# A decoder trunk on one core: the gated-attention projections of heads 1 to 3 in pairs of column strips, seven block products to a pair

## The reference, cut to what matters

```python
proj = rmsnorm(h, norm_g) @ w_in                  # 1024 -> q 1024, k 1024, v 2048, gate 16, r 2048
log_a = log_sigmoid(g_low @ w_gate_up + b_gate) / 16
# 4 heads: q, k, log_a (528, 256), v and r (528, 512) each; chunked causal attention:
b = cumsum(log_a)                                  # inside a chunk
attn = where(causal, (q * exp(b)) @ (k * exp(-b)).T, 0)
o = attn @ v + (q * exp(b)) @ S                    # S carries the chunks before
y = rmsnorm(o per head) * head_norm_g * silu(r)
h = h + y @ w_out
```

## Time and profile before

| | |
|---|---|
| time, median of 2 runs | 1004.57 us (1004.5 to 1004.64) |
| span of the profiled execution | 1002.4 us |
| TensorE busy | 994.3 us, 99% of the span, 7843 instructions |
| VectorE busy | 732.4 us, 73% |
| ScalarE busy | 552.2 us, 55% |
| GpSimd busy | 90.6 us, 9%, all of it after the GLA layer |
| DMA | 107.69 MB, mean 107 GB/s |

### The profile page before, as it was taken

One profiled execution on the slowest core, in us unless ns is written; L12 is line 12 of the kernel. 1 busy time (PEld: TensorE's weight loads), 2 busy tenths in 40 slices (PEclk: granted clock), 3 DMA queues, 4 the chain that ended last, 5 costly groups with the idle time before them and its releaser, 6 DMA issues.

```text
span 1002.4 us, 19364 instructions
## 1 busy us (share of the span) xinstructions
PE 994.3 (99%) x7843; PEld 940.7 (94%) x7843; DVE 732.4 (73%) x1190; ACT 552.2 (55%) x915; POOL 90.6 (9%) x97
## 2 busy tenths in 40 slices
PE   9999999999999999999999999999999999999998
PEld 8999999999999999998889989999899989988897
DVE  6874677477567875435889976898589966989875
ACT  6754654564465554334566655656366645566633
POOL 0000000000000000000232211222112211210000
PEclk9999999999999999999999999999999999999999
DMA  8221231132122113333334432444244533486332
GB/s 293 78 71 64 67 101 45 63 103 68 64 72 97 44 63 127 105 108 104 113 82 122 108 137 60 134 103 137 89 114 110 120 117 91 124 257 233 115 106 84
DMA packets 42392, 107.69 MB, mean 107 GB/s; under 512 B 4784, under 2 KB 12848, under 8 KB 42304
## 3 DMA queue, kind: packets, MB, share of 16 engines
q1 hardware_dynamic: 41584, 105.78, 34.6%
q10 hardware_dynamic: 720, 0.68, 0.2%
HBM read 98.34 MB, written 7.90 MB: 106 GB/s over the span
## 4 chain that ended last, share of the span: by engine, by line
PE 89%; DVE 6%; ACT 2%; issue 2%; DMA 0%; DVEq 0%; ACTq 0%
PE psum L2076 50%; PE psum L2452 13%; PE psum L2371 7%; PE psum L2430 3%; PE psum L2566 3%; PE psum L2201 2%; DVE w_lo L1226 1%; PE psum L2411 1%; PE psum L2149 1%; PE psum L2573 1%; PE psum L2197 1%; PE psum L2399 1%; PE psum L2398 1%; PE psum L2400 1%; PE psum L2170 1%
## 5 line engine op out<-in xcount | busy, mean ns | idle before, releaser
L1226 DVE TENSOR_TENSOR w_lo<-raw,w_hi 128x1024 fp32r<-128x1024 f32 x156 | 191.5, 1242 | 38.3 <-ACT w_hi L682 28.0
L682 ACT ACTIVATE w_hi<-raw 128x1024 fp32r<-128x1024 f32 x156 | 162.9, 1052 | 47.8 <-PE psum L2371 29.5
L2076 PE MATMUL psum<-xh,w_hi 128*128 128x264 f32 x768 | 159.1, 288 | 0.2 <-DVE w_lo L1240 0.2
L2076 PE MATMUL psum<-xl,w_hi 128*128 128x264 f32 x768 | 155.9, 285 | 0.0
L2076 PE MATMUL psum<-xh,w_lo 128*128 128x264 f32 x768 | 155.2, 283 | 0.0
L2076 PEld LDWEIGHTS psum<-xh,w_hi 128*128 128x128 f32 x768 | 118.6, 189 | 1.6 <-issue 1.4
L2076 PEld LDWEIGHTS psum<-xl,w_hi 128*128 128x128 f32 x768 | 119.5, 188 | 0.0
L2076 PEld LDWEIGHTS psum<-xh,w_lo 128*128 128x128 f32 x768 | 119.1, 189 | 0.0
L624 POOL TENSOR_TENSOR sub<-sub,cst 128x128 f32<-128x128 f32 x64 | 50.8, 796 | 650.1 <-DMA sub<-sums 649.8
L2076 PE MATMUL psum<-y_lo,w_hi 128*128 128x264 f32 (+2 forms) x336 | 79.6, 299 | 0.0
L2452 PE MATMUL psum<-y_lo,w_hi 128*128 128x256 f32 x312 | 57.9, 287 | 0.1
(11 more groups left out here) (353 smaller groups left out, 2486.5 us busy)
## 6 DMA issues: line engine op xcount, KB each, us to landing
raw<-w_all SPq DMA_DIRECT2D x143, 512.0 KB, 3.5
sub<-sums SPq DMA_DIRECT2D x16, 264.0 KB, 7.2
y_keep<-sq SPq DMA_DIRECT2D x14, 256.0 KB, 2.2
y<-y_keep SPq DMA_DIRECT2D x14, 256.0 KB, 6.5
sub<-sums SPq DMA_DIRECT2D x16, 200.0 KB, 6.3
yr<-y_keep SPq DMA_DIRECT2D x12, 256.0 KB, 4.9
sub<-sums SPq DMA_DIRECT2D x16, 136.0 KB, 4.9
hT<-xT SPq DMA_DIRECT2D x8, 264.0 KB, 5.3
```

The costliest lines, as they stand in the source:

```text
L682: nc.scalar.activation(w_hi[:, n % HI_RING, :], raw[:, n % LO_RING, :], ACT.Copy).then_inc(hi_made, 1)
L1226: nc.vector.tensor_tensor(w_lo[:, n % LO_RING, :], raw[:, n % LO_RING, :], w_hi[:, n % HI_RING, :].bitcast(F32), ALU.subtract).then_inc(lo ...
L2076: i = nc.tensor.matmul(o, w[a][:, k % KT, :], x[b][:, k, c0:c1], start=k == first and a == b == 0, stop=k == last and a == 1)
```

## The change

Heads 1 to 3 no longer take their 36 strips one by one. Two strips form a pair (18 pairs: q, k, v, r, w, s of each head, where w and s are the second halves of v and r), and a pair's product is seen as a 2 x 2 block product: the two strips, the two halves of the 1024 features, the two halves of the tokens. Seven block products (`gp`, 4 k-tiles x 3 parts = 12 matmuls of 264 columns each) take the place of eight. Their order on TensorE is 1, then 3 of the pair before, then 2, 6, 5, 7, 4.

- **Tokens.** At the end of head 0 VectorE scales `hT` in place by gain and `rstd` (`norm_tokens`), makes four sums or differences of its quarters (`token_sum`), and ScalarE and VectorE split the quarters and the sums anew. `xT` is loaded again after the last product, as `hT` no longer holds the residual stream.
- **Weights.** Of a pair, chunks `a` and `b` are loaded; four half chunks (s1 to s4) are sums, made by DMAs of GpSimd's queue that add what they read to what lies at their destination (`pair_sums`). s1 has a buffer of its own, s3 lies in chunk `b`, and s2 and s4 make up chunk `e`, which is split like the others. ScalarE splits `e` right behind the first copy of the pair, `keep(n, 0)`.
- **Outputs.** Products 1, 6 and 7 add up in one PSUM bank, and ScalarE copies it after each of them (`keep` 0, 1, 2); 5 and 3 add up in another. VectorE makes the four output quarters (`pair_out`), each an addition of one PSUM bank and one copy.
- **Scaling.** q, k, v and r need no `rstd` any more; the 1/16 of q moves into the head's root. v's split is one instruction each instead of four.
- The order of ScalarE, VectorE and TensorE in heads 0 to 3 is rewritten around the pairs. TensorE's product `A{h}3` moves into the next head's first pair, for head 3 into the output projection.

```diff
+GP = [(x, h) for h in range(1, GLA_HEADS) for x in "qkvrws"]
+GP_STRIPS = {"q": ("Q", 0, 1), "k": ("K", 0, 1), "v": ("V", 1, 0), "r": ("R", 1, 0), "w": ("V", 3, 2), "s": ("R", 3, 2)}
+GP_BANK = {1: 2, 6: 2, 7: 2, 2: 3, 5: 0, 3: 0, 4: 1}
+GP_ORDER = []
+for _n in range(len(GP)):
+    GP_ORDER += [(1, _n)] + ([(3, _n - 1)] if _n else []) + [(p, _n) for p in (2, 6, 5, 7, 4)]
+GP_ORDER += [(3, len(GP) - 1)]
+GP_AT = {x: i + 1 for i, x in enumerate(GP_ORDER)}
...
+        GP_X = {1: (part_of(xh, 0, 0), part_of(xl, 0, 0)), 2: (part_of(xh, 1, 0), part_of(xl, 1, 0)), 3: (part_of(xh, 1, 1), part_of(xl, 1, 1)),
+                5: (th[:, 0], part_of(tl, 0, 0)), 6: (th[:, 1], part_of(tl, 0, 1)), 7: (th[:, 2], part_of(tl, 1, 0)),
+                4: (part_of(xh, 0, 1), part_of(tl, 1, 1))}
...
+                    a = w_all[AT[f"p{n:02d}a"]]
+                    s2, s4 = pair_raw(n, "e")
+                    if n == 1:
+                        sp.wait_ge(strip_made, 8)
+                        sp.wait_ge(xn_made, KT)
+                    elif n:
+                        sp.wait_ge(prod_done, GP_AT[(5, n - 2)])
+                    if n:
+                        sp.wait_ge(s1_sum, 16 * n)
+                    sp.dma_start(gs1(n)[0], w_all[AT[f"p{n:02d}b"], :, 0:CH // 2]).then_inc(s1_loaded, 16)
+                    if n < 2:
+                        wait_chunk_used(sp, m - 1 - LO_RING)
+                    else:
+                        sp.wait_ge(prod_done, GP_AT[(6, n - 2)])
+                    if n:
+                        sp.wait_ge(s2_sum, 16 * n)
+                    sp.dma_start(s2, a[:, 0:CH // 2]).then_inc(s2_loaded, 16)
+                    load(m)
+                    if n >= 2:
+                        wait_chunk_used(sp, m - 1 - LO_RING)
+                    if n:
+                        sp.wait_ge(s4_sum, 16 * n)
+                    sp.dma_start(s4, a[:, CH // 2:CH]).then_inc(s4_loaded, 16)
...
+                pool.wait_ge(s1_loaded, 16 * (n + 1))
+                pool.dma_start(s1_, from_b[:, CH // 2:CH], accum_op=ALU.add).then_inc(s1_sum, 16)
+                pool.wait_ge(s2_loaded, 16 * (n + 1))
+                pool.wait_ge(s1_sum, 16 * (n + 1))
+                pool.dma_start(s2, s1_, accum_op=ALU.add).then_inc(s2_sum, 16)
+                pool.wait_ge(w_loaded[b % LO_RING], 16 * LOADS[b])
+                if n:
+                    pool.wait_ge(s3_sum, 16 * n)
+                pool.dma_start(s3, from_a[:, 0:CH // 2], accum_op=ALU.add).then_inc(s3_sum, 16)
+                pool.wait_ge(s4_loaded, 16 * (n + 1))
+                pool.wait_ge(s2_sum, 16 * (n + 1))
+                pool.dma_start(s4, s2, accum_op=ALU.add).then_inc(s4_sum, 16)
...
+            def keep(n, i):
+                act.wait_ge(prod_done, GP_AT[((1, 6, 7)[i], n)])
+                if n:
+                    act.wait_ge(out_made, gp_out_at(n - 1, ("11", "12", "21")[i]))
+                nc.scalar.activation((u1, u2, u3[:])[i], bank(GP_BANK[1], 0, HALF), ACT.Copy, scale=(1.0, 1.0, -1.0)[i]).then_inc(copied, 1)
...
+                    n = pair("v", h)
+                    keep(n, 0)
+                    if n:
+                        pair_high(n, "e")
+                    pair_high(n, "b")
+                    decay_kb(h)
+                    decay_qb(h)
+                    keep(n, 1)
+                    pair_high(n + 1, "a")
+                    s1_high(n + 1)
+                    decays_last(h)
...
+                n = pair("w", h)
+                keep(n, 0)
+                if n:
+                    pair_high(n, "e")
+                gla_scores_hi(h)
                 gla_gate(h, 1)
-                gla_scores_hi(h)
-                ahead(f"V{h}2")
-                gla_value(h, 2)
+                pair_high(n, "b")
+                pair_high(n + 1, "a")
+                keep(n, 1)
+                s1_high(n + 1)
...
+                product, u, i = {"11": (2, u1, 0), "22": (5, u3[:], 2), "21": (4, u3[:], 2), "12": (3, u2, 1)}[name]
+                dve.wait_ge(copied, 3 * n + i + 1)
+                dve.wait_ge(prod_done, GP_AT[(product, n)])
...
+                    pair_low(n + 1, "a")
+                    pair_low(n + 1, "e")
+                    s1_low(n + 1)
+                    difs_last(h)
+                    n = pair("v", h)
+                    pair_out(n - 1, "12")
+                    pair_low(n, "b")
+                    pair_out(n, "11")
+                    mul_q64(h)
+                    first_low(n + 1)
+                    pair_out(n, "22")
+                    pair_out(n, "21")
+                    pair_low(n + 1, "a")
+                    pair_low(n + 1, "e")
+                    s1_low(n + 1)
+                    mul_qj(h)
+                    half_inverse(h - 1, 0)
+                    n = pair("r", h)
+                    pair_out(n - 1, "12")
+                    pair_low(n, "b")
+                    pair_out(n, "11")
+                    half_inverse(h - 1, 1)
+                    mul_qc(h)
+                    gla_values_lo(h, 0)
+                    muls_far(h)
+                    muls_k(h)
...
+                    head_row(h - 1, 0)
+                    head_row(h - 1, 1)
+                pair_low(n + 1, "a")
+                pair_low(n + 1, "e")
+                s1_low(n + 1)
+                if h + 1 == GLA_HEADS:
+                    y_low(0)
+                n = pair("s", h)
                 gla_out(h, 0)
...
+                x = GP_X[product]
+                o = bank(GP_BANK[product], 0, HALF)
+                for k in range(KT // 2):
+                    for a, b in PARTS:
+                        i = nc.tensor.matmul(o, w[k][a], x[b][:, k, :], start=product not in (3, 6, 7) and k == a == b == 0,
+                                             stop=k == KT // 2 - 1 and a == 1,
+                                             skip_group_check=product in (3, 6, 7))
+                i.then_inc(prod_done, 1)
...
+                    for x in "kvr":
+                        n = pair(x, h)
+                        gp(1, n)
+                        gp(3, n - 1)
+                        if x == "k":
+                            head_sum(h - 1)
+                        gp(2, n)
+                        gp(6, n)
+                        if x == "r":
+                            gla_transposed(h, 0)
+                        gp(5, n)
+                        gp(7, n)
+                        gp(4, n)
                 gla_scores(h)
...
+                n = pair("s", h)
+                gp(1, n)
+                gp(3, n - 1)
+                gp(2, n)
                 gla_attend(h, 1)
                 gla_transposed(h, 2)
-                strip(f"V{h}3", x1)
+                gp(6, n)
+                gp(5, n)
                 gla_attend(h, 2)
                 gla_transposed(h, 3)
-                strip(f"R{h}3", x1)
-                gla_attend(h, 3)
-                if h + 1 < GLA_HEADS:
-                    gate_logits(h + 1, 0)
+                gp(7, n)
+                gp(4, n)
```

More of the change, by code:

```diff
@@ L166 @@
     _last[_area] = _job
-CHUNKS = ([c for h in range(GLA_HEADS) for c in gla_strips(h)] + [f"W{d}{half}" for d in range(KT) for half in "ab"]
+CHUNKS = (FIRST_STRIPS + [c for n in range(len(GP)) for c in pair_chunks(n)] + [f"W{d}{half}" for d in range(KT) for half in "ab"]
           + ["k0", "u00", "u01", "u02", "u03", "k1", "q0"] + [x for h in range(FOX_HEADS) for x in fox_chunks(h)]
@@ L261, in program @@
         acc = sb("acc", [P, T])
-        rstd = sb("rstd", [P, T])
+        with ExitStack() as one:
+            rstd = sb("rstd", [P, T], F32, one)
+        rstd_lo = sb("rstd_lo", [P, T], F32R)
         rtok = sb("rtok", [P, NBLK + 1])
@@ L581, in _ @@
                     spread_sums(spread[n])
+                if n == CHUNK["W2b"]:
+                    sp.wait_ge(prod_done, len(GP_ORDER))
+                    for d in range(KT):
+                        sp.dma_start(hT[:, d, :], xT[:, d, :]).then_inc(h_loaded[d], 16)
                 if n in keep:
@@ new lines, in _ @@
+                    gla_gate(0, 0)
+                    gla_gate(0, 1)
+                    gla_scores_hi(0)
+                    ahead("V02")
+                    gla_value(0, 2)
+                    gate_abs(1, 0)
+                    gate_abs(1, 1)
+                    gate_exp(1)
+                    gla_square(0, 0)
+                    gla_values_hi(0, 1)
+                    gate_log(1)
+                    split(CHUNK["p00a"])
+                    gla_gate(0, 2)
+                    gla_square(0, 1)
@@ L885, in _ @@
+                if h + 1 < GLA_HEADS:
+                    gate_exp(h + 1)
+                else:
+                    y_high(0)
+                n = pair("s", h)
                 gla_square(h, 0)
                 gla_values_hi(h, 1)
-                ahead(f"R{h}2")
+                keep(n, 0)
+                if n:
+                    pair_high(n, "e")
+                if h + 1 < GLA_HEADS:
+                    gate_log(h + 1)
```

(47 more changed lines are left out.)

830 lines of the change are left out of this document (615 added, 215 removed).

## The result

The changed kernel takes **1044.05 us** (median of 2 runs, 1043.52 to 1044.58), before 1004.57: ratio 1.0395, 95% interval 1.0365 to 1.0426. It is 39.5 us slower; I forecast 19.4 slower. The time lies inside the range, at its upper end, where the rival of the DMA chain begins; the change is twice the one forecast.

What follows compares the result with a forecast made beforehand. TensorE, busy 99% of the span, was taken as the bound: 1002.4 - 26.3 saved + 33.0 waits + 9.2 start of head 1 + 3.7 end of head 3 = 1022.0, plus 2.2 for the median: 1024 us; range 998 to 1045.

Steps and rivals of the forecast that it cites:

- the rival of the DMA chain: All pairs: adding DMAs of 5 to 6 us set the pair's length, 1042 to 1060 us in total; chance 0.2.
- Saved: Heads 1 to 3, TensorE: 216 fewer matmuls at 0.1217 us, 26.3 us less, 8.76 per head.
- VectorE's load: Per head: rises from 58 to 69 of some 80 us, so its sum doesn't become the bound.
- The waits by order: Heads 1 to 3: TensorE waits on the feeding engines' in-order queues, 11.0 us per head, 33.0 in all.
- product 5, r pair: TensorE waits 1.87 us while VectorE does qj and half a reciprocal before the output quarter.
- scores: TensorE waits 2.2 us before the scores, for VectorE's chain ending in product kb.
- w pair and neighbours: `keep(n, 1)` comes late behind e's split and the scores' copies: 1.4 us, 2.5 with waits around it.
- `A{h}1`, s pair: TensorE waits 2.4 us before `A{h}1` for v's split, which stands behind e and s1.
- v pair (head 1, where the DMAs don't hide it): Product 5 waits 0.66 us behind a difference of the decays, product 7 another 0.33 for its copy.
- Start of head 1: Token sums, splits and other VectorE work delay the first pair: 10.1 us less 0.9 counted elsewhere, +9.2.
- End of head 3: `A31` 2.4 us later behind y's low parts, a copy 0.4, the head sum 0.9: +3.7 us.
- an adding DMA may take about 4 us: Pair's DMA chain has 14.6 us and 0.4; each adding DMA taken as 3.5 us, costed at nothing.

Runs made afterwards that it cites:

- x1_no_sums: Changed kernel without GpSimd's adding DMAs, plain loads standing in for the sums, so products use weights that aren't the sums: 1029.5 us, ratio 1.025.
- x2_plain: Changed kernel with its four GpSimd DMAs kept in order and with their waits, but copying without adding: 1035.8 us, ratio 1.030.
- x3_third: Changed kernel with a third buffer for s1, its load ahead of chunk a and waiting for product 5 of three pairs back: 1047.2 us, ratio 1.0437.

## Why the prediction was off, step by step

- **Saved**: 216 matmuls at their pace, right. A product's matmuls follow at 0.12 us at full clock, so 12 to one bank run as a strip's do.
- **VectorE's load**: 70 us per head against 69 forecast, right. Its operations take the same beside 181 GB/s (w_lo 1.22, s 1.22).
- **The waits by order.** Head 2 of the changed kernel, from the distances of its products' starts less 1.46 us and the known work between them (for product 5 of the r pair: 250.21 - 246.47 - 1.46 - 0.46 = 1.83):

| wait | forecast | measured |
|---|---|---|
| product 5, r pair | 1.87 | 1.83 |
| scores | 2.2 | 2.2 |
| w pair and neighbours | 2.5 | 2.5 |
| `A{h}1`, s pair | 2.4 | 2.3 |
| v pair (head 1, where the DMAs don't hide it) | 1.0 | 1.05 |
| q and small | 0.95 | 0.6 |

 Sizes right; one releaser wrong. (The v pairs of heads 2 and 3 have the chain's wait in their place.) The waits view adds up to 42.8 us of idle TensorE in heads 1 to 3 where I had 46, with some 12 of the DMA chain in it: restarts and matmuls at the lower clock don't count as idle, so starts are the better ruler. In the w pair product 7 waits for VectorE's low part of b (0.85 idle), whose high part stands behind the scores on ScalarE, not for `keep(n, 1)`.
- **Start of head 1**: forecast 9.2, made of 8.7 up to product 3 of the first pair and 1.4 before the next product 6, less 0.9 counted elsewhere. (Its terms for VectorE add up to 20.8 us, not 20.4, and give 8.8.) Up to that product 3 TensorE loses 2.27 us before its first product, then 1.90, 1.69 and 2.64, 8.5 in all. The 1.4 didn't come as a wait; behind the last of these the clock is at its lower level and costs 1.6. **End of head 3**: `A31` waits 4.6 us (forecast 4.8 with the y splits), then runs at the lower clock.
- All of this without the DMA chain is x1_no_sums: forecast 1024, measured 1029.5, and 1026.5 in its run with the best clock.
- **The step that failed** is "an adding DMA may take about 4 us; ... I take 3.5 and cost it at nothing". It takes 3.8 (s2) to 5.3 us (s3) to landing and 5 to 6 to the issue of the next link, and the chain 20.1 us instead of 15. So the term that I put at nothing measures 14.5 us, of the 20 missing: 1044.05 - 1029.5. I took the 512 KB load as the nearest row; it has no second issue by GpSimd behind it and nothing to wait for. The quoted estimate of the Trainium skill, "DMA: Bandwidth & Descriptors", 2.6 us for 256 KB, doesn't agree with the trace either: 3.3 and 4.1 for the DMAs of x2_plain that only copy.
- **The DMA rival** held in its mechanism: links of 5 to 6 us, over the 4 from which it decides, make product 6 wait. It didn't hold in its place or its price. I expected all pairs alike. The chain of pair n has ten products' time, 14.6 us, only where nothing else stands between them; a head's attends (2.3 us each) and scores (5.3) lengthen it everywhere but ahead of the v and the r pair. Of these two one pays per head: where the v pair has waited, the r pair's chain has had that time too, and product 6 of the r pair starts without a wait (246.47 in head 2). In head 1 it is the r pair that waits, behind the late start, and in x3_third, where the v pairs hardly wait, the r pairs do. So the chain costs 14.5 us where the rival had 18 to 36, and that the total falls into its 1042 to 1060 is partly luck: 5.5 us more come from elsewhere.
- **The clock** has no term in the sum, though the forecast itself makes TensorE wait, which it hardly did before. Five waits in the changed kernel (2.4 and 3.9 us in head 1, 4.2 in head 2, 4.3 and 4.6 in head 3) are followed by matmuls at 0.22 us: 2.5 us more behind each v pair's wait in heads 2 and 3 (in head 2 start distances 2.80 and 2.64 instead of 1.46). The estimate of 6 us for x1_no_sums covers the rest, the 5.5 us between 1024 and 1029.5; it is read from one trace and from the runs' clocks, not isolated by an experiment.
- FoX, forecast the same to 0.5 us: from TensorE's first matmul with the tile `zh` (at 493.8 of 1041.7 us, before at 455.6 of 1002.4) to the end of the span 547.9 us against 546.8. The other versions lie between 546.4 and 548.0, so this is no effect of the change that can be told.

## What to carry to other kernels

A chain of dependent DMAs is priced by its depth: count the links, take each at the time from issue to the next issue (here 5 to 6 us for 256 KB; half the bytes took only 1.1 to 1.2 us off the landing), and compare the sum with the shortest stretch of work between the buffer's release and its next use. When a product becomes smaller, walk the in-order queues of the engines that feed it; that walk gave the waits here to a few tenths, and moving four groups of instructions by its account took out 20 us without the sums and 10 with them. An engine that never waited can lose twice when it starts to: the wait and the slower clock behind it.
